# Two decoder layers without a loop: one program for both, with the memory's blocks of layer 1 in the end of layer 0

## The chip, the core and the metric

The kernel runs on one core of a Trainium2 chip. Its engines each run their own instruction stream and meet only through semaphores: TensorE (PE; its weight loads are listed as PEld), VectorE (DVE), ScalarE (ACT), GpSimd (POOL, used here for DMA issues only) and SyncE (SP, DMA issues only). The metric is the device time of one launch in microseconds (us).

## What is computed

The reference is one step of a hybrid decoder trunk of DEPTH = 2 layers, for 256 prompt tokens and 8 sample tokens together (264 columns). Cut to what matters for the change, one layer is

```
h = x @ w_in                                  # 2048 -> 19024 columns, split among the branches
mk, mv = split(mem_prompt @ w_mem_kv)         # 256 memory tokens; mem_prompt is the same in both layers
y_e = attention(mem_q, mk, mv) * silu(mem_z)  # needs mk, mv; the other branches don't
y_a .. y_d = delta net, sparse attention, retention, LRU, each times silu of its gate path
merged = sum over branches of sigmoid(gate_b) * (y_b @ w_branch[b])
out = merged @ w_out
x = LayerNorm(1.414 * x + out)                # over the 2048 features; the next layer's x
```

x of layer 0 is the input, the last x is the main output, and each layer also stores caches and states. What layer 1 needs of layer 0 is x alone; mk and mv of layer 1 need only mem_prompt and the weights.

## The kernel before

**Stages.** The program has three parts in a row: a small block that brings x in (lines 500 to 537), a hardware loop over the two layers (Fori, line 541) whose body is one block for all engines, and a small block that puts x out (lines 2133 to 2164). Between them, and at the end of each pass of the loop, stands clear_sems (line 491): all engines meet, the DMA queues are reset, all semaphores are set to zero, and all meet again. No weight of layer 1 is asked for before that.

**The stream of chunks.** The work of a layer is a list, CHUNKS (plan(), line 84), in one order for all engines: 4 chunks of mem_q (MQ), 2 "narrow", 8 "mem" (the products with w_mem_kv), then the other projections, the gates, and 16 "out" chunks (w_out). A chunk is one 128-wide column block against all 2048 rows, in 16 k-steps. x is held in features by tokens (xsplit) as a high and a low part in a rounded type, weights likewise (wsplit), and a k-step of an ordinary chunk is three products, lines 619 to 621. Before them ACT rounds a half of the weight block (line 1158) and DVE takes the rest (line 1404); SP loads the halves into a ring of four (line 572) as slots come free. A mem chunk takes its weights from the ring as they are, as float32: lines 608 (keys, 4 chunks) and 611 (values, 4 chunks). Its input memT is mem_prompt with features down, made in each layer by 32 transposes on PE (line 701) from a 2 MB load (memrow, line 1214), issued by ACT.

**The order on each engine** is written out by hand: fill(n) runs the next n k-steps of the stream on PE between the small products of a branch, stream(n) the next n chunks; ACT and DVE have stream calls of their own that prepare weights for the next chunk and empty the result banks. PSUM has four banks for the stream (mb) and four for the branches (bb).

**End of a layer.** After the last out chunk PE sums the new x over features with 16 products against ones (line 1130), DVE subtracts the mean (line 2006), ACT squares (line 1371), PE sums the squares (line 1135), ACT takes the root (line 1373), DVE the reciprocal (line 2009), DVE scales (line 2011), ACT writes the high part of the next x (line 1376) and DVE the low part (line 2015).

**Start and end of the program.** x comes in by SP: all constant tables (1551.5 KB), x_prompt (2048 KB), x_sample and the page table, then 48 transposes (lines 518 and 519), each group of three emptied by ACT and DVE. The last block adds the two parts of x (line 2150), transposes in 12 groups of four (line 2144), copies (line 2156) and stores from SP (lines 2161 and 2163).

Of the kernel before, what the change touches and what calls it, by code (L numbers as in the profile page):

```python
# [83 lines left out]
def plan():  # L84
# [20 lines left out]
CHUNKS = plan()  # L105
# [21 lines left out]
MEMKV_READY, NARROW_READY = (FREED[FIRST_RESULT[max(i for i, x in enumerate(CHUNKS) if x[0] == kind)]][1]  # L127
                             for kind in ("mem", "narrow"))


# [20 lines left out]
def kv_count(n, i):  # L151

    g = 4 if i % NKV >= 2 else 0
    return 16 * (i // NKV + 1) if n == 0 else 16 * (4 + g) + 32 * (i // NKV + 1)


def gath_count(j):

    return 16 * (4 + j // 2 + 1)


def ready(slot):

    return FREED[FIRST_RESULT[CHUNKS.index(("in", slot, CPS - 1))]][1]


# [82 lines left out]
def trunk(nc, a, o, at, fixed_w):  # L249

    n_pool = a.cache_dsa_k.shape[1]
    with ExitStack() as ctx:
# [51 lines left out]
        r1 = area(RK, 0, D)  # L304
        r2 = area(DQ, 0, W)
        memrow = area(GQ, 0, 2 * D).rearrange("p (t n) -> p t n", t=2)
        memT = area(DK, 0, KC * NMEM).rearrange("p (c n) -> p c n", n=NMEM)
        xrow = memrow
        pti = area(DK, 0, 1 + NB * NPG).bitcast(I32)
# [5 lines left out]
        def hi(ap):  # L315

            return ap.bitcast(F32R)
# [26 lines left out]
        lcount = sm(1)  # L344
# [84 lines left out]
        def kvb(n, b):  # L429
# [39 lines left out]
            ln_sum ln_cen ln_sq ln_ss ln_rs ln_x y_out se_ok mean_ok memv_out lc_ok decays_in v_chain a_chain  # L469
            cp_out""".split()  # L470
# [8 lines left out]
        layer_sems = kv_in[0:2] + list(sem) + w_landed + bw_landed + gath + stin  # L479

# [10 lines left out]
        def clear_sems():  # L491
            nc.all_engine_barrier()
            nc.gpsimd.dma_reset()
            nc.all_engine_barrier()
            for i, s in enumerate(layer_sems):
                (nc.sync, nc.scalar, nc.tensor, nc.vector)[i % 4].sem_clear(s)
            nc.all_engine_barrier()


        with nc.Block() as block:  # L500
            @block.sync
            def _(sp):
                sp.dma_start(tab[:, :], a.fixed).then_inc(sem.tables, 16)
                sp.dma_start(xrow, a.x_prompt.rearrange("a (t p) n -> p (a t) n", p=P)).then_inc(sem.x_in, 16)
                sp.dma_start(r1[0:NB, :], a.x_sample.rearrange("b t n -> (b t) n")).then_inc(sem.x_in, 16)
                pt = a.page_table.rearrange("b g -> (b g)")
                sp.dma_start(pti[:, 0:1], pt.rearrange("(p o) -> p o", o=1)).then_inc(sem.pages_in, 16)
                sp.dma_start(pti[:, 1:], pt.partition_broadcast(P)).then_inc(sem.pages_in, 16)

            @block.tensor  # L510
            def _(pe):
                pe.wait_ge(sem.tables, 16)
                pe.wait_ge(sem.x_in, 32)
                for c in range(KC):
                    if c >= 4:
                        pe.wait_ge(sem.x_ok, c - 3)
                    for t in range(2):
                        pe.transpose(mb[:, c % 4, t * P:(t + 1) * P], xrow[:, t, c * P:(c + 1) * P], ident)
                    pe.transpose(mb[:, c % 4, NP:T], r1[0:NB, c * P:(c + 1) * P], id8).then_inc(sem.x_T, 1)

            @block.scalar
            def _(act):
                for c in range(KC):
                    act.wait_ge(sem.x_T, c + 1)
                    act.activation(hi(xsplit[:, 0, c, :]), mb[:, c % 4, 0:T], ACT.Copy).then_inc(sem.xh_ok, 1)
# [1675 lines left out]
```

## Time and profile before

| | us |
|---|---|
| median of 3 runs (3160.26 to 3162.92) | 3162.58 |
| the profiled execution | 3162.21 |
| its span, first to last instruction | 3160.4 |
| PE busy | 2932.9 |
| DVE busy | 1705.0 |
| ACT busy | 974.4 |

The profile is of one execution, and sums are made against its 3162.2 us; it stands 0.4 us from the median. Busy time of PE is the union of its matmul intervals, which overlap one another; a float32 product of 256 columns stands as two records.

### The profile page before, as it was taken

The numbers are of one execution on the slowest core, as the hardware profiler recorded it, in microseconds if no ns is written. First come the engines' busy times: TensorE is split into PE (matmuls) and PEld (weight loads), VectorE is DVE, ScalarE is ACT, GpSimd is POOL, SyncE is SP. The second block draws the span as 40 slices with busy tenths as digits, with TensorE's granted clock in tenths as the row PEclk, the third lists the DMA queues.
The fourth block names the chain that finished last, engine by engine and source line by source line (L and its number), as shares of the span: only waits on it lengthen the run. The fifth ranks groups of instructions, "written<-read, shape, count | busy, mean of one in ns | idle before, by whom it ended". The sixth has DMA issues, their size and how long they took to land. (4 is left out here: it accounts for less than half of the span.)

```text
span 3160.4 us, 52449 instructions
## 1 busy us (share of the span) xinstructions
PE 2932.9 (93%) x21616; PEld 2752.6 (87%) x21616; DVE 1705.0 (54%) x2464; ACT 974.4 (31%) x1301; POOL 181.4 (6%) x204
## 2 busy tenths in 40 slices
PE   6999988999999999999779999899999999999995
PEld 5988888998999898899779888789898999989994
DVE  3155376656566747444422644765666657554444
ACT  2133332223252332223313333322233423322242
POOL 0000000000000003100000010000100000040000
PEclk9998999999999999999989999999999999999998
DMA  5576444465656567665257654444656564586651
GB/s 174 149 206 183 130 110 108 115 163 139 176 158 163 146 169 208 181 174 167 67 154 201 184 169 120 121 109 115 171 156 161 155 179 135 156 238 170 171 162 39
DMA packets 830708, 485.98 MB, mean 154 GB/s; under 512 B 26052, under 2 KB 812612, under 8 KB 829218
## 3 DMA queue, kind: packets, MB, share of 16 engines
q1 hardware_dynamic: 809328, 410.00, 48.1%
q0 software_dynamic: 19840, 66.75, 6.8%
q10 hardware_dynamic: 1296, 5.80, 0.5%
q8 instruction: 174, 2.85, 0.4%
q14 instruction: 70, 0.57, 0.1%
HBM read 466.27 MB, written 16.47 MB: 153 GB/s over the span
## 5 line engine op out<-in xcount | busy, mean ns | idle before, releaser
L619 PE MATMUL mb<-xsplit,wsplit 128*128 128x264 f32 (+1 forms) x5312 | 1580.9, 298 | 83.1 <-DVE wsplit L1404 75.9
L620 PE MATMUL mb<-xsplit,wsplit 128*128 128x264 f32 (+1 forms) x5312 | 1529.6, 288 | 0.0
L621 PE MATMUL mb<-xsplit,wsplit 128*128 128x264 f32 (+1 forms) x5312 | 1527.9, 288 | 0.0
L619 PEld LDWEIGHTS mb<-xsplit,wsplit 128*128 128x128 f32 (+1 forms) x5312 | 1022.6, 193 | 121.2 <-issue 56.0
L620 PEld LDWEIGHTS mb<-xsplit,wsplit 128*128 128x128 f32 (+1 forms) x5312 | 1022.6, 193 | 8.1 <-issue 3.8
L621 PEld LDWEIGHTS mb<-xsplit,wsplit 128*128 128x128 f32 (+1 forms) x5312 | 1016.2, 191 | 1.1
L1404 DVE TENSOR_TENSOR wsplit<-ring,wsplit 128x1024 fp32r<-128x1024 f32 (+2 forms) x664 | 776.8, 1209 | 265.8 <-ACT wsplit L1158 253.1
L1158 ACT ACTIVATE wsplit<-ring 128x1024 fp32r<-128x1024 f32 (+2 forms) x664 | 662.9, 1043 | 144.0 <-PE mb L621 99.9
L1185 ACT ACTIVATE gbuf<-mb 128x264 f32<-128x264 f32 x160 | 62.4, 390 | 840.2 <-PE mb L621 827.4
L635 PE MATMUL mb<-work,bring 128*128 128x264 f32 x1280 | 310.6, 385 | 0.0
L1434 DVE TENSOR_TENSOR gbuf<-gbuf,mb 128x264 f32<-128x264 f32 x128 | 54.8, 428 | 431.7 <-PE mb L635 424.2
L635 PEld LDWEIGHTS mb<-work,bring 128*128 128x128 f32 x1280 | 231.3, 189 | 31.6
L1199 ACT ACTIVATE work<-mb 128x264 f32<-128x264 f32 x136 | 52.8, 388 | 567.2 <-PE mb L621 562.1
L1438 DVE SCALAR_TENSOR_TENSOR work<-work,mb 128x264 f32<-128x264 f32 x32 | 13.7, 429 | 101.2 <-PE mb L621 101.2
L1688 DVE SCALAR_TENSOR_TENSOR work<-bb,mws 128x1024 f32<-128x1024 f32 x16 | 19.6, 1224 | 74.0 <-PE bb L851 74.0
L1435 DVE TENSOR_TENSOR merged<-merged,gbuf 128x264 f32<-128x264 f32 x128 | 55.4, 433 | 4.4
L611 PEld LDWEIGHTS mb<-ring,work 128*128 128x128 f32 x512 | 57.5, 192 | 0.1
L611 PE MATMUL mb<-ring,work 128*128 128x128 f32 x512 | 57.5, 275 | 0.0
L2050 POOL DMA_INDIRECT work<-in_cache_dsa_k_dram,rowsU x32 | 38.0, 1189 | 311.6 <-DVE rowsU L1997 301.3
L608 PE MATMUL mb<-work,ring 128*128 128x256 f32 x256 | 55.6, 379 | 0.0
L608 PEld LDWEIGHTS mb<-work,ring 128*128 128x128 f32 x256 | 48.5, 190 | 6.5
L749 PE MATMUL bb<-work,tab 8*128 8x512 f32 x64 | 40.6, 742 | 10.2 <-DVE work L1574 10.2
(446 smaller groups left out, 2262.6 us busy)
## 6 DMA issues: line engine op xcount, KB each, us to landing
ring<-in_w_in_dram SPq DMA_DIRECT2D x592, 512.0 KB, 4.6
bring<-in_w_branch_dram SPq DMA_DIRECT2D x160, 256.0 KB, 3.1
ring<-in_w_out_dram SPq DMA_DIRECT2D x64, 512.0 KB, 4.1
ring<-in_w_mem_kv_dram SPq DMA_DIRECT2D x32, 512.0 KB, 3.6
work<-in_cache_mem_k_dram POOLq DMA_DIRECT2D x16, 512.0 KB, 5.4
work<-in_cache_mem_v_dram POOLq DMA_DIRECT2D x16, 512.0 KB, 4.5
work<-in_mem_prompt_dram ACTq DMA_DIRECT2D x2, 2048.0 KB, 11.7
work<-in_state_gdn_dram POOLq DMA_DIRECT2D x8, 512.0 KB, 6.4
```

What stands on the lines that cost most here:

```text
L608: mm = pe.matmul(bank[:, 0:NMEM], w, memT[:, q, :], start=first, stop=last)
L611: mm = pe.matmul(bank[:, t * P:(t + 1) * P], memT[:, q, t * P:(t + 1) * P], w, start=(first and t == 0), stop=last, skip_group_check=True)
L619: pe.matmul(bank[0:n, 0:T], wh, ah, start=first, stop=False)
L620: pe.matmul(bank[0:n, 0:T], wh, al, start=False, stop=False)
L621: mm = pe.matmul(bank[0:n, 0:T], wl, ah, start=False, stop=last)
L635: mm = pe.matmul(mb[:, (g + 1) % 4, 0:T], bring[:, j % 2, q, :], y[:, q, :], start=(q == 0), stop=(q == CPS - 1))
L1158: act.activation(hi(wsplit[:, s % 4, 0, :, 0:n]), ring[:, p % NRING, :, 0:n], ACT.Copy)\
L1185: act.activation(gbuf[:, :], src[:, 0:T], ACT.Sigmoid).then_inc(sem.gate_act, 1)
L1199: act.activation(H(x)[:, m, :], src[:, 0:T], ACT.Silu if x in (GZ, DZ, RZ, LZ, MZ) else ACT.Copy).then_inc(sem.stored, 1)
L1404: dve.tensor_tensor(hi(wsplit[:, s % 4, 1, :, 0:n]), ring[:, p % NRING, :, 0:n], wsplit[:, s % 4, 0, :, 0:n], ALU.subtract).then_inc(sem.l ...
L1434: v(dve.tensor_tensor(gbuf[:, :], gbuf[:, :], proj, ALU.mult))
L1435: dve.tensor_tensor(merged[:, m, :], merged[:, m, :], gbuf[:, :], ALU.add).then_inc(sem.merged_ok, 1)
```

## The change

The two layers are written one after the other in one block, with no loop, no meeting of the engines and no clearing of semaphores: every wait gets a count that goes on over both layers (K[l], base). The two blocks that brought x in and out are parts of the same block now. CHUNKS is the list of both layers, and the 8 mem chunks are the first of each layer.

In layer 0, mem_prompt is loaded first, by SP, right behind the first 128 columns of the tables (the identity matrix); the rest of the tables follows behind the first four weight loads. x is loaded by ACT. PE transposes mem_prompt, then x, with four k-steps of mem chunks behind each group of x. At the end of layer 0, mem_prompt is loaded again behind ACT's first out chunk; its 32 transposes stand behind out chunk 3, in eight groups with four k-steps of out chunks behind each; the 16 sums of x each stand three chunks behind; and mem chunks of layer 1 (6 k-steps, then 3 behind each group of squares) stand within the norm. The last x isn't split; ACT writes it in place, PE transposes each quarter as it comes, and POOL stores it in five DMAs.

```
+    chunks.extend(("mem", 0, m) for m in range(2 * CPS))
     project(MQ)
     chunks.extend(("narrow", 0, m) for m in range(2))
-    chunks.extend(("mem", 0, m) for m in range(2 * CPS))
...
-CHUNKS = plan()
+LEN = len(plan())
+CHUNKS = plan() * DEPTH
...
-        with nc.Fori(0, DEPTH) as l:
...
+                sp.dma_start(tab[:, 0:P], a.fixed[:, 0:P]).then_inc(sem.tab_id, 16)
+                sp.dma_start(memrow, a.mem_prompt.rearrange("a (t p) n -> p (a t) n", p=P)).then_inc(sem.mem_in, 16)
...
+                        if i == 1:
+                            sp.dma_start(tab[:, P:], a.fixed[:, P:]).then_inc(sem.tables, 16)
...
+                        if kind == "mem" and m == 0:
+                            pe.wait_ge(sem.memT_ok, K[l].memT_ok + 8)
...
+                                if i % LEN == 2 * CPS:
+                                    pe.wait_ge(sem.x_ok, KC * l + q + 1)
...
+                def bring_memory(l):
+                    pe.wait_ge(sem.mem_in, K[l].mem_in + 16)
+                    for t in range(2):
+                        for q in range(4):
...
+                            for c in range(4):
+                                mm = pe.transpose(bb[:, n % 4, c * P:(c + 1) * P],
+                                                  memrow[:, t, (4 * q + c) * P:(4 * q + c + 1) * P], ident)
+                            mm.then_inc(sem.mem_T, 1)
+                            if l:
+                                fill(4)
+                bring_memory(0)
+                pe.wait_ge(sem.x_in, 32)
+                for c in range(KC):
+                    pe.wait_ge(*((sem.memT_ok, c + 5) if c < 4 else (sem.x_ok, c - 3)))
+                    for t in range(2):
+                        pe.transpose(bb[:, c % 4, t * P:(t + 1) * P], xrow[:, t, c * P:(c + 1) * P], ident)
+                    pe.transpose(bb[:, c % 4, NP:T], xsrow[:, c * P:(c + 1) * P], id8).then_inc(sem.x_T, 1)
+                    fill(4)
+                pe.wait_ge(sem.x_ok, KC)
+                pe.wait_ge(sem.tables, 16)
...
-                    stream(None)
-                    pe.wait_ge(sem.out_ok, KC)
+                    out_0 = (l + 1) * LEN - KC
+                    stream_to(out_0 + 4)
+                    if l + 1 < DEPTH:
+                        bring_memory(l + 1)
+                        pe.wait_ge(sem.memT_ok, K[l + 1].memT_ok + 8)
                     for q in range(KC):
-                        mm = pe.matmul(bb[:, 0, 0:T], ones, xnew[:, q, :], start=(q == 0), stop=(q == KC - 1))
+                        stream_to(min(out_0 + q + 3, out_0 + KC))
+                        pe.wait_ge(sem.out_ok, KC * l + q + 1)
+                        mm = pe.matmul(bb[:, 0, 0:T], ones, xnew[:, q, :], start=(q == 0), stop=(q == KC - 1),
+                                       skip_group_check=True)
                     mm.then_inc(sem.ln_sum, 1)
+                    fill(6)
                     for q in range(4):
...
                         mm.then_inc(sem.ln_ss, 1)
+                        fill(3)
+                n = 0
+                for q in range(4):
+                    pe.wait_ge(sem.xh_ok, base.xh_ok + 4 * q + 4)
...
# ACT, head of each layer
+                    stream(4)
+                    act.wait_ge(sem.x_ok, KC * (l + 1))
+                    act.wait_ge(sem.cols_ok, 1)
+                    params(l)
+                    stream(2 * CPS)
# ACT, end of each layer
+                    stream_to(out_0 + 1)
+                    if l + 1 < DEPTH:
+                        act.dma_start(memrow, a.mem_prompt.rearrange("a (t p) n -> p (a t) n", p=P)).then_inc(sem.mem_in, 16)
+                    stream_to(out_0 + KC)
# DVE, end of each layer
+                    stream_to(out_0 + 4)
+                    if l + 1 < DEPTH:
+                        bring_memory(l + 1)
+                    stream_to(out_0 + KC)
# POOL, end of the program
+                for q in range(4):
+                    pool.wait_ge(sem.x_ok, base.x_ok + 3 * q + 3)
+                    c = slice(q * 512, (q + 1) * 512)
+                    pool.dma_start(y_prompt[:, :, c], yrow[:, :, c]).then_inc(sem.y_out, 16)
+                pool.dma_start(o.y_sample.rearrange("b t n -> (b t) n"), ysrow[0:NB, :]).then_inc(sem.y_out, 16)
```

In the rows that follow, xN is a count of equal instructions, and the bracket holds the semaphores that the instruction waits for. PE at the start of the program before: the transposes of x, the meeting point (ISA, 39 semaphore clears), and the first products with weights.

```order
L518 MATMUL mb<-tab,work 128x128 [waits x_in,tables]
L518 MATMUL mb<-tab,work 128x128
L519 MATMUL mb<-tab,work 128x8
...
L496 ISA x38
L541 UNCONDITIONAL_BRANCH [waits barrier_Pool_Activation_PE_DVE_SP_release]
L584 UNCONDITIONAL_BRANCH
L619 MATMUL mb<-xsplit,wsplit 128x264 [waits lo_ok]
```

The same place now: L657 are transposes of mem_prompt, L669 and L670 of x, L596 the k-steps of mem chunks.

```order
L657 MATMUL bb<-tab,work 128x128 [waits mem_in,tab_id]
L657 MATMUL bb<-tab,work 128x128 x15
...
L669 MATMUL bb<-tab,work 128x128 [waits memT_ok,x_in]
L669 MATMUL bb<-tab,work 128x128
L670 MATMUL bb<-tab,work 128x8
L596 MATMUL mb<-work,ring 128x256 [waits w_landed0,memT_ok]
L596 MATMUL mb<-work,ring 128x256 x3
```

The mem chunks moved from behind the narrow ones to between the groups of x, and the meeting point is gone. PE at the end of layer 0 before: the sums of x (L1130), the sums of squares (L1135), the meeting point.

```order
L1130 MATMUL bb<-work,tab 128x264 [waits out_ok]
L1130 MATMUL bb<-work,tab 128x264 x15
L1135 MATMUL bb<-work,tab 128x264 [waits ln_sq]
L1135 MATMUL bb<-work,tab 128x264 x3
...
L553 UNCONDITIONAL_BRANCH
L496 ISA [waits barrier_Pool_Activation_PE_DVE_SP_release]
L496 ISA x38
```

The same place now: three of the 16 sums (L1146) are left behind the last out chunk, and k-steps of mem chunks of layer 1 (L596) stand behind them and behind each group of squares (L1153).

```order
L1146 MATMUL bb<-work,tab 128x264 [waits out_ok] x3
L596 MATMUL mb<-work,ring 128x256 [waits w_landed0,out_ok,memT_ok]
L596 MATMUL mb<-work,ring 128x256 x5
L1153 MATMUL bb<-work,tab 128x264 [waits ln_sq]
L1153 MATMUL bb<-work,tab 128x264 x3
L596 MATMUL mb<-work,ring 128x256 x2
L596 MATMUL mb<-work,ring 128x256 [waits w_landed1]
```

ACT at the same place now: behind the last scaling of x (L1431) it empties four mem chunks (L1224) ahead of the loads of the parameters, which wait for all of x.

```order
L1427 ACTIVATE work<-bb,tab 128x264 [waits ln_ss]
L1431 ACTIVATE xsplit<-work,pT 128x264 [waits ln_x] x16
L1224 ACTIVATE memkv<-mb 128x256 [waits chunk_mm] x4
L1240 DMA work<-in_conv_w_dram 4x2048 [waits cols_ok,x_ok]
L1242 DMA work<-in_conv_b_dram 1x2048
```

Before, the meeting point stood behind the scaling, and behind it the first loads and roundings of weights.

## Rows read from the trace of the kernel before

**Rows 1.** The page: span, PE's busy time, the queue of PE's instructions (packets, MB, share).
```profile
span 3160.4 us, 52449 instructions
PE 2932.9 (93%) x21616; PEld 2752.6 (87%) x21616; DVE 1705.0 (54%) x2464; ACT 974.4 (31%) x1301; POOL 181.4 (6%) x204
...
q8 instruction: 174, 2.85, 0.4%
```

**Rows 2.** Who PE waited for: total us, times, longest.
```profile
PE mb L619 <- DVE wsplit L1404: 75.9, 18, 33.4
PE mb L2144 <- DVE work L2150: 26.7, 1, 26.7
```

**Rows 3.** Timeline of PE, start: start us, us, operation, [idle before <- releaser].
```profile
13.52 0.66 PE L518 MATMUL mb<-tab,work 128*128 128x128 f32 x2 [13.52 <-DMA work<-in_x_sample_dram]
...
40.31 0.59 PE L619 MATMUL mb<-xsplit,wsplit 128*128 128x264 f32 x1 [13.63 <-DVE wsplit L1404]
```

**Rows 4.** DMA from 0 to 34 us in 40 equal slices: rate.
```profile
GB/s 0 0 146 190 380 438 409 398 410 414 434 424 453 292 82 22 0 0 0 0 0 0 0 0 0 0 0 0 0 0 0 0 0 0 0 0 0 10 10 0
```

**Rows 5.** DMA issues from 34 to 80 us: KB each, median us to landing.
```profile
ring<-in_w_in_dram SPq DMA_DIRECT2D x8, 512.0 KB, 6.2
work<-in_mem_prompt_dram ACTq DMA_DIRECT2D x1, 2048.0 KB, 11.8
```

**Rows 6.** Busy time by stretch, layer 0's head: length, PE busy (x), others, clock, DMA.
```profile
40.31:65.69 25.38, 25.38 (x192) 25.24 (x192) 8.85 (x9) 8.09 (x12) 0.00 (x0) 1.00 1.05 283
65.69:72.81 7.12, 7.12 (x69) 5.58 (x69) 2.31 (x4) 1.53 (x3) 0.00 (x0) 1.00 0.51 143
72.81:76.40 3.59, 3.59 (x34) 3.38 (x33) 2.95 (x5) 0.38 (x1) 0.00 (x0) 1.00 0.25 62
76.40:82.27 5.87, 5.87 (x52) 5.87 (x50) 1.92 (x4) 0.00 (x0) 0.00 (x0) 1.00 0.00 0
82.27:109.89 27.62, 27.62 (x130) 24.32 (x129) 0.00 (x0) 1.54 (x4) 0.00 (x0) 1.00 0.45 133
109.89:138.48 28.59, 28.59 (x258) 28.59 (x257) 3.06 (x6) 3.65 (x6) 0.00 (x0) 1.00 0.52 147
138.48:151.11 12.63, 12.63 (x106) 12.42 (x104) 3.08 (x4) 6.07 (x7) 0.73 (x1) 1.00 0.89 230
```

**Rows 7.** Timeline of POOL and DVE, first stores of the memory's keys in layer 0.
```profile
146.53 0.73 POOL L2028 DMA_DIRECT2D out_p_mem_k_dram<-stg  x1 [145.82 <-DVE stg L1535]
...
151.78 0.69 DVE L1535 COPY stg<-bb 128x512 f32<-128x512 f32 x1 [6.03 <-DMA out_p_mem_k_dram<-stg]
```

**Rows 8.** Timeline from layer 0 to layer 1: PE, then DVE and SP.
```profile
1546.40 7.39 PE L1130 MATMUL bb<-work,tab 128*128 128x264 f32 x32 [0.52 <-DVE work L1438]
1556.25 9.07 PE L1135 MATMUL bb<-work,tab 128*128 128x264 f32 x32 [2.46 <-ACT work L1371]
1598.74 0.59 PE L619 MATMUL mb<-xsplit,wsplit 128*128 128x264 f32 x1 [33.42 <-DVE wsplit L1404]
...
1574.18 6.55 DVE L2015 SCALAR_TENSOR_TENSOR xsplit<-work,pT,xsplit 128x264 fp32r<-128x264 f32 x16
...
1590.73 13.56 SPq L572 DMA_DIRECT2D ring<-in_w_in_dram  x8
```

**Rows 9.** PE in 5.8 us behind two equal waits: length, busy (records), clock, DMA.
```profile
1452.84:1458.64 5.80, 5.80 (x48) 1.00 0.01 2
3004.72:3010.52 5.80, 5.80 (x26) 0.50 0.00 1
```

**Rows 10.** Timeline of the program's end: DVE, SP, PE.
```profile
3120.72 6.55 DVE L2011 SCALAR_TENSOR_TENSOR work<-work,pT 128x264 f32<-128x264 f32 x16
...
3150.44 4.36 DVE L2156 COPY work<-mb 128x512 f32<-128x512 f32 x7 [0.16 <-PE mb L2144]
...
3152.45 0.40 SPq L2161 DMA_DIRECT2D out_y_prompt_dram<-work  x1
...
3145.02 8.26 PE L2144 MATMUL mb<-tab,work 128*128 128x128 f32 x48 [26.69 <-DVE work L2150]
```

More of the change, by code:

```diff
@@ L489, in chain, with at_l @@
             return link
[L491 to L497, printed above, removed]
+        K = [counts(l) for l in range(DEPTH)]
+        def at_l(ap, l):
+            n = len(ap.shape)
+            rest = " ".join(f"x{i}" for i in range(1, n))
+            return ap[l:l + 1].rearrange(f"z {rest} -> (z x1) " + " ".join(f"x{i}" for i in range(2, n)))
         with nc.Block() as block:
@@ L502, in _ @@
             def _(sp):
[L503 to L519, printed above, removed]
@@ new lines, in _, with weights @@
+                sp.dma_start(memrow, a.mem_prompt.rearrange("a (t p) n -> p (a t) n", p=P)).then_inc(sem.mem_in, 16)
+                def weights(l):
+                    w = {"mem": a.w_mem_kv, "out": a.w_out, "in": a.w_in}
+                    w = {name: at_l(ap, l).rearrange("(k p) n -> p k n", p=P) for name, ap in w.items()}
+                    return w, at_l(a.w_branch, l).rearrange("b (k p) n -> p b k n", p=P)
+                for l in range(DEPTH):
+                    by_kind, w_branch = weights(l)
+                    for i, (kind, x, m) in list(enumerate(CHUNKS))[l * LEN:(l + 1) * LEN]:
@@ L562, in _ @@
                             n = P
-                        w = {"mem": w_mem, "out": w_out}.get(kind, w_in)
+                        w = by_kind.get(kind, by_kind["in"])
                         for h in range(2):
@@ L805, in _ @@
                     mm.then_inc(sem.gt_mm, 1)
-                    pe.wait_ge(sem.gt_ok, 1)
+                    pe.wait_ge(sem.gt_ok, base.gt_ok + 1)
                     def rotate(n, slot, mat):
-                        pe.wait_ge(sem.stored, ready(slot))
+                        pe.wait_ge(sem.stored, ready(l, slot))
                         for c in range(CPS):
@@ new lines, in _ @@
+                        fill(3)
+                n = 0
+                for q in range(4):
+                    pe.wait_ge(sem.xh_ok, base.xh_ok + 4 * q + 4)
+                    for t in range(3):
+                        m = P if t < 2 else NB
+                        if n >= 4:
+                            pe.wait_ge(sem.x_ok, base.x_ok + n - 3)
+                        for c in range(4):
+                            mm = pe.transpose(mb[0:m, n % 4, c * P:(c + 1) * P], xnew[:, 4 * q + c, t * P:t * P + m], ident)
+                        mm.then_inc(sem.x_T, 1)
+                        n += 1
@@ new lines, in _ @@
+                act.dma_start(xrow, a.x_prompt.rearrange("a (t p) n -> p (a t) n", p=P)).then_inc(sem.x_in, 16)
+                pt = a.page_table.rearrange("b g -> (b g)")
+                act.dma_start(pti[:, 0:1], pt.rearrange("(p o) -> p o", o=1)).then_inc(sem.pages_in, 16)
+                act.dma_start(pti[:, 1:], pt.partition_broadcast(P)).then_inc(sem.pages_in, 16)
+                for c in range(KC):
+                    act.wait_ge(sem.x_T, c + 1)
+                    act.activation(hi(xsplit[:, 0, c, :]), bb[:, c % 4, 0:T], ACT.Copy).then_inc(sem.xh_ok, 1)
@@ L1216, in _ @@
+                for l in range(DEPTH):
+                    base = K[l]
                     stream(4)
+                    act.wait_ge(sem.x_ok, KC * (l + 1))
+                    act.wait_ge(sem.cols_ok, 1)
+                    params(l)
+                    stream(2 * CPS)
                     stream(2)
-                    stream(8)
                     stream(2)
@@ L1892, in _ @@
                     normed(4, RQ)
-                    dve.wait_ge(sem.stored, ready(RZ))
+                    dve.wait_ge(sem.stored, ready(l, RZ))
                     dve.tensor_tensor(H(RZ), H(RZ), H(RQ), ALU.mult).then_inc(sem.yc_ok, 1)
```

1026 lines of the change are left out of this document (505 added, 521 removed).

## The prediction

> **What bounds the kernel now.** I read the page's busy line first: PE is busy 2932.9 of 3160.4 us, no other engine over 54% [rows 1]. So the question is when PE stands still, and the list of PE's waits answers it: most of them are 1 to 6 us inside the layers, and three are not. 33.4 us of the wait for rounded weights is one wait, and 26.7 us another [rows 2]. The timelines place them. From 0 to 40.3 us PE does nothing but 48 transposes of x: 13.5 us until x has landed and 13.6 us between the last of them and the first weights [rows 3]. From layer 0 to layer 1 the last out chunk ends at 1546.40 - 0.52 = 1545.9 and the first chunk of layer 1 starts at 1598.7, 52.9 us in which PE has two runs of sums, 7.4 and 9.1 us [rows 8]; x is complete at 1580.7, and the meeting point takes from there to 1590.7, when SP asks for the first weights. At the end of the program x is scaled at 3120.72 + 6.55 = 3127.3, and the span ends at 3160.4 [rows 1, 10]. The change aims at these three places and at little else, so I sum each place as a path on PE, before and after.
>
> **Start, up to the first attention of layer 0.** Before, PE is ready for it at 151.1 and starts when the second row copy is done, 151.78 + 0.69 = 152.5 [rows 6, 7]. After, the path is:
> - First transpose. Before, tables and x (1551.5 + 2048 + 64 + 64 KB) landed by 13.5 at some 0.42 MB per us [rows 3, 4]. After, identity and memory (64 + 2048 KB) go by SP and x_sample and x (64 + 2048 KB) by ACT at the same time. If the queues share evenly, 0.5 MB more than before are in front: 13.5 + 1.2 = 14.7. If the memory comes first: 2.16 MB / 0.42 = 5.1, with some 2.9 us before the rate is reached, about 8.0. Rows 5 are the nearest: the memory on ACT's queue took 11.8 us beside weights on SP's, that is, it shared. I take 14.7.
> - The Trainium skill, page "DMA: Bandwidth & Descriptors", section "Queues, rings and completion order", has each DMA engine go round-robin between the queues with work, a packet at a time. By it loading x on a second queue buys the memory nothing, and the sum would be 14.7 too; by memory first the end would be 6.7 us earlier. No row here shows two large loads alone on two queues.
> - 32 transposes of the memory at the end block's pace of 8.26 / 48 = 0.17 us (the half clock) [rows 10]: 5.5, and 0.7 for DVE's last copy. 20.9.
> - 64 k-steps of the key chunks, 27.6 [rows 6], with 48 transposes of x between them at 3.59 / 32 = 0.11, 5.4, and the half clock at the first dense work, 25.4 - 4 x 5.8 = 2.2, as the first four chunks had it [rows 6]. 56.1. ACT and DVE emptied 16 such groups of x before in 40.31 - 13.52 - 13.63 = 13.2 us, 0.8 a group [rows 3], and now have 33 / 16 = 2.1; ACT empties the banks before it waits for x and issues the parameters, so nobody is queued behind those.
> - Value chunks 28.6, four MQ chunks 23.2, parameters and narrow chunks 7.1 + 5.9, rows and two MZ chunks 12.6 [rows 6]: 133.5.
> - The copy that PE waited for before hangs on a store of 5.3 to 6.0 us behind a late weight split [rows 7]. After, the chunk before it is a narrow one, whose weights are small and early, so the copy comes before PE needs it; I take its 1.4 us as gone.
> Gain 152.5 - 133.5 = 19.0 us.
>
> **Layer 0 to layer 1.** Before: 52.9 us from the last out chunk to MQ, and from MQ to the attention as in layer 0, 152.5 - 40.3 = 112.2; together 165.1. After, nothing of PE's work goes, it is put elsewhere: 32 transposes, 3.6, and 13 of 16 sums at 7.39 / 16 = 0.46, 6.0, stand among the out chunks, which are bound by PE, so both lengthen that stage by their own time. Behind the last chunk 3 sums, 1.4 (DVE's 0.5 lies beside two of them). Then the squares 7.4 and all 8 mem chunks 56.2, MQ 23.2 without the half clock, 7.1 + 5.9 + 12.6. Sum 3.6 + 6.0 + 1.4 + 7.4 + 56.2 + 48.8 = 123.4. Gain 41.7 us.
>
> It holds if the norm is covered. From the end of the first sums, 1553.8, to x complete took 26.9 us [rows 8]; the k-steps put between the squares make that about 29. PE reaches MQ, the first that needs x, only after 7.4 + 56.2 = 63.6. The four stream banks are the nearer limit: PE can run four mem chunks, 27.6 + 7.4 = 35, before ACT must have emptied one, and ACT is free when it has scaled x: DVE's low parts, the step behind, began 1574.2 - 1553.8 = 20.4 after the sums [rows 8], with the k-steps put between about 23. Cover left: some 12 us; each us beyond that costs one. What else is moved: the 2 MB load is issued about one out chunk into the stage, 11.8 us to land [rows 5], and PE wants it three to four chunks, 17 to 23 us, later; beside weights at 512 KB per 2.9 us the weights will be slowed, as they were to 6.2 us in rows 5, where PE didn't wait either. DVE gets 8 copies of about 0.65 us [rows 10] in two out chunks of 5.8 us, beside its own rounding there. I cost both at nothing; without cover the copies are 5 us and the load 2 to 3 us.
>
> **End.** Up to the scaling all is as before, but 0.5 us earlier (7.9 us for wait and sums become 6.0 + 1.4). Before, 3160.4 - 3127.3 = 33.1 us follow: low parts, meeting point, sum of parts, transposes, copies, one 2 MB store. After, PE transposes each quarter while DVE still scales, so 12 copies at 0.62 to 0.69 [rows 10] follow, 7.9, then on POOL two issues of 0.73 and a landing; 256 KB by POOL took 5.3 [rows 7], the last 512 KB and x_sample may take 4 to 8. 7.9 + 1.5 + 5.3 = 14.7. Gain 33.1 - 14.7 + 0.5 = 18.9.
>
> **Sum.** 19.0 + 41.7 + 18.9 = 79.6; 3162.2 - 79.6 = 3082.6, against a profiled time that stands 0.4 below the median. I say 3083. Unknown sizes: the landing at the start, 7 less or 1 more; the last store, 1 less or 3 more; the half clock within the layers. Two equal waits of 3.6 us were followed by 48 products in 5.8 us at the full clock in one layer, and by 26 at half in the other [rows 9], so a shift of all later work deals these stretches anew, each worth some 5.8 x 22 / 48 = 2.7 us; I take it as 0, plus or minus 10 (four stretches either way).
>
> **Rivals.**
> - The start runs cold, or starves. Before, PE stayed at the half clock through the 13 us of x's transposes, and transposes now stand between the k-steps. If that whole stage stays at half, 27.6 + 5.4 = 33 become 66 less the 2.2 counted: 3083 + 31 = 3114. Against: PE has no gap there, and in the first four chunks dense work warmed it within 25.4 us at a loss of 2.2 [rows 6]. Late weights behind the memory would cost up to 5: 3088. Price range 3098 to 3115.
> - More than I count: the memory lands first (6.7), the end's store lands early (1), and the anew dealt half clock comes out well (8): 3083 - 16 = 3067.
> - Slower than before. A straight program has twice the instructions to be brought in from memory. If the loop's second pass found its code on the core, PE's 174 loads of code would be more than before, and from 79.6 / 174 = 0.46 us of stall at each the gain is lost; at 1 us each the time is 3083 + 174 = 3257. Against: 2.85 MB over PE's 2 x 21616 matmul and weight instructions is 66 bytes each [rows 1], so both passes are brought in already, and PE still is busy 93%.
> - It doesn't do what it says: a wait left in the order ties layer 1's mem chunks to x, and the norm stays bare. Then the middle gain shrinks to the meeting point and the weights, 10 + 8 us, and the time is 3083 + 24 = 3107. In the order of the new kernel the mem chunks wait for banks, weights and memT alone, so little speaks for it.
>
> **How the numbers follow.** Forecast (3070 to 3097) 0.65; start costs more or norm partly bare (3097 to 3120) 0.16; more (3055 to 3070) 0.14; slower 0.03; within 0.2% of before 0.02. 0.2%, 6.3 us, is about what a measurement of this kernel can tell from no change. Likeliest 3083; the range reaches from 3063 to 3107. Faster 0.95, same 0.02, slower 0.03.
>
> **What the new profile would show.** Right: first transpose at 14 to 15 us; PE's first MQ chunk at about 85; no wait of PE over 2 us between the last out chunk of layer 0 and MQ of layer 1, with 56 us of mem chunks there; x of layer 1 complete some 30 us before MQ asks for it; the span ending 14 to 16 us after the last scaling. Wrong: PE at the half clock over most of the start, a wait of PE for stored or for the memory's landing at the layers' border, or more time in the middle of a layer than before, where the change moves nothing.

## The result

The changed kernel takes 3084.5 us (median of 4 runs, 3081.6 to 3087.0) against 3162.2 before: a ratio of 0.9755, 95% interval 0.9738 to 0.9772. The forecast was 3083, range 3063 to 3107. The page of the profile after, to set beside [rows 1]:

```profile
span 3081.8 us, 49873 instructions
...
PE 2923.6 (95%) x21616; PEld 2746.5 (89%) x21616; DVE 1693.9 (55%) x2442; ACT 970.3 (31%) x1299; POOL 184.6 (6%) x209
...
q8 instruction: 171, 2.80, 0.4%
```

PE has the same 21616 matmuls, its busy time fell by 9.3 us, and the span by 78.6. So some 69 us are time in which PE stood still. The code loaded on q8, PE's by its size, didn't grow (171 packets against 174), though the program is written out twice. Who PE waited for, after (us in total, times, longest):

```profile
PE mb L609 <- DVE wsplit L1459: 27.8, 14, 3.1
...
PE bb L657 <- DMA work<-in_mem_prompt_dram: 13.8, 1, 13.8
...
PE mb L1166 <- ACT work L1431: 4.7, 1, 4.7
```

The 33.4 and 26.7 us of [rows 2] are gone; what is left for rounded weights is 14 waits of at most 3.1 us inside the layers. Cut at the same places in both traces, the span moves like this:

| stretch (us) | before | after | gain | forecast |
|---|---|---|---|---|
| start to first attention of layer 0 | 152.5 | 134.8 | 17.7 | 19.0 |
| on to the first out chunk of layer 0 | 1300.3 | 1299.7 | 0.6 | 0 |
| on to the first attention of layer 1 | 258.7 | 216.1 | 42.6 | 41.7 |
| on to the first out chunk of layer 1 | 1293.2 | 1294.5 | -1.3 | 0 |
| on to the last scaling of x | 122.6 | 122.1 | 0.4 | 0.5 |
| on to the span's end | 33.1 | 14.5 | 18.6 | 18.4 |
| sum | 3160.4 | 3081.8 | 78.6 | 79.6 |

The stretches are differences of starts and ends in PE's and DVE's timelines.

**Start.** The timeline of PE, then the queues from 0 to 14 us (packets, MB, share of time):

```profile
13.84 6.45 PE L657 MATMUL bb<-tab,work 128*128 128x128 f32 x32 [13.84 <-DMA work<-in_mem_prompt_dram]
...
21.24 1.99 PE L596 MATMUL mb<-work,ring 128*128 128x256 f32 x8 [0.57 <-DVE work L1505]
...
86.02 0.37 PE L609 MATMUL mb<-xsplit,wsplit 128*128 128x264 f32 x1
```

```profile
q1 hardware_dynamic: 620, 2.27, 44.1%
q10 hardware_dynamic: 437, 2.17, 38.9%
```

Up to the landing of the memory SP's queue (q1) and ACT's (q10, the one with x) had moved the same amount: the two loads shared. PE was at its first MQ product at 86.0, where it had been at 40.3, but with all eight mem chunks behind it.

**Border.** Windows of PE by stage (length, PE busy and instructions, the other engines, clock, DMA): key chunks at the start, out chunks of layer 0, norm, key chunks and value chunks of layer 1, MQ.

```profile
20.13:57.52 37.39, 36.82 (x178) 29.72 (x177) 8.11 (x20) 7.07 (x19) 0.00 (x0) 1.00 0.48 151
...
1434.52:1537.14 102.62, 102.52 (x826) 101.46 (x827) 49.13 (x56) 33.01 (x32) 0.00 (x0) 1.00 0.60 172
1537.14:1552.22 15.08, 15.08 (x71) 12.84 (x70) 5.18 (x5) 5.61 (x5) 0.00 (x0) 1.00 0.12 36
1552.22:1573.37 21.15, 21.15 (x100) 18.62 (x98) 14.82 (x33) 8.00 (x20) 0.00 (x0) 1.00 0.50 150
1573.37:1601.87 28.50, 28.50 (x257) 28.50 (x256) 2.45 (x2) 3.58 (x6) 0.00 (x0) 1.00 0.62 176
1601.87:1625.26 23.39, 23.39 (x196) 23.25 (x194) 7.63 (x8) 7.87 (x12) 0.00 (x0) 1.00 0.78 186
```

PE is busy from the first out chunk to MQ without a wait and at the full clock, where [rows 8] had 33.4 us of nothing. ACT there:

```profile
1555.30 6.60 ACT L1431 ACTIVATE xsplit<-work,pT 128x264 fp32r<-128x264 f32 x16 [2.40 <-DVE work L2090]
1561.81 0.62 ACT L1224 ACTIVATE memkv<-mb 128x256 f32<-128x256 f32 x2
...
1573.57 0.38 ACT L1224 ACTIVATE memkv<-mb 128x256 f32<-128x256 f32 x1 [6.52 <-PE mb L596]
```

ACT has emptied the first bank by 1562.1, and PE wants it at 1573.4, when the fifth mem chunk begins: a cover of 11.3 us.

**End.** DVE's scaling and copies, then POOL's last stores:

```profile
3060.73 6.56 DVE L2090 SCALAR_TENSOR_TENSOR work<-work,pT 128x264 f32<-128x264 f32 x16
3067.20 7.31 DVE L2103 COPY work<-mb 128x512 f32<-128x512 f32 x12
...
3074.80 0.72 POOL L2224 DMA_DIRECT2D out_y_prompt_dram<-work  x1 [1.08 <-DVE work L2103]
3075.52 0.55 POOL L2225 DMA_DIRECT2D out_y_sample_dram<-work  x1
```

7.2 us of copies, 1.6 of issues and waits, 5.7 from the last issue to the span's end, 14.5 together. Of the 5.7, the trace's semaphore records give 3.1 to the landing of the last store, at 3079.1. The other 2.7 lie behind it: POOL is in a DRAIN instruction, which no view counts as busy, at the end of its program until 3081.6, and the other engines wait for it there.

### The profile page after: what moved, and what is told of

It reads as the page before. It is cut to its first block, busy times and chain, and to the rows that moved or that the text cites. A ratio compares the mean times of both kernels' runs of the same rounds, so it can differ in the third digit from the quotient of the medians.

```text
span 3081.8 us, 49873 instructions
## 1 busy us (share of the span) xinstructions
PE 2923.6 (95%) x21616; PEld 2746.5 (89%) x21616; DVE 1693.9 (55%) x2442; ACT 970.3 (31%) x1299; POOL 184.6 (6%) x209
## 4 chain that ended last, share of the span: by engine, by line
PE 81%; DVE 14%; ACT 3%; issue 1%; DMA 1%; POOL 0%; DVEq 0%; POOLq 0%; ACTq 0%; SPq 0%
PE mb L609 18%; PE mb L610 18%; PE mb L611 18%; PE mb L625 8%; DVE wsplit L1459 3%; PE mb L596 2%; PE mb L599 2%; DVE work L1817 1%; PE bb L1024 1%; PE bb L863 1%; PE bb L868 1%; PE bb L760 1%; DVE work L1807 1%; PE bb L971 1%; ACT wsplit L1190 1%
## 5 line engine op out<-in xcount | busy, mean ns | idle before, releaser
L596 PE MATMUL mb<-work,ring 128*128 128x256 f32 x256 | 60.3, 386 | 0.6 <-DVE work L1505 0.6
L596 PEld LDWEIGHTS mb<-work,ring 128*128 128x128 f32 x256 | 47.3, 190 | 6.8 <-DVE work L1505 0.7
```

The costliest lines, as they stand in the source:

```text
L596: mm = pe.matmul(bank[:, 0:NMEM], w, memT[:, q, :], start=first, stop=last)
```

## The experiments

The question after such a result is whether the sum came out for its own reasons. Each kernel was timed beside the kernel before (medians 3162.0 to 3164.6). Runs of one kernel spread over 2 to 13 us, so effects of a few us are read from the stage of the profile that they concern.

### The straight program alone

The order of the chunks and the k-steps put between x's groups, the sums and the squares are undone; the single program is kept.

```
-    chunks.extend(("mem", 0, m) for m in range(2 * CPS))
     project(MQ)
     chunks.extend(("narrow", 0, m) for m in range(2))
+    chunks.extend(("mem", 0, m) for m in range(2 * CPS))
...
-                    fill(4)
...
-                    fill(6)
...
-                        fill(3)
```

> The straight program alone: the mem chunks go back behind the narrow ones in both layers, nothing of the stream stands between the groups of x at the start nor in the norm; one program, early loads, the transposes of the memory and the new end stay. Theory: at the start x takes 8.4 us behind the memory's transposes, then 112.2 - 3.6 us to the first attention, 138 to 140 against 134.8, 4 to 5 later; at the border MQ starts with the first low parts of x, about 22 us behind the last out chunk, and 108.6 plus 1 for DVE's pace plus 2 to 3 for the half clock follow, 133 to 136 against 113.6, 20 to 22 later. Sum 24 to 27 us slower than the changed kernel, so that the order of the mem chunks is worth about a third of the gain and the straight program two thirds. Rival (the meeting point and the late weights are small beside the norm): 40 us and more slower.

Measured: 3109.6 us (3107.0 to 3111.8), 25.1 slower than the changed kernel. PE at the start and at the border:

```profile
32.24 0.56 PE L609 MATMUL mb<-xsplit,wsplit 128*128 128x264 f32 x1 [2.99 <-DVE wsplit L1456]
...
1566.54 0.56 PE L609 MATMUL mb<-xsplit,wsplit 128*128 128x264 f32 x1 [9.49 <-DVE xsplit L2092]
```

MQ starts 20.8 us behind the last out chunk, at its first low part of x; the first attention of layer 1 comes 130.6 behind it against 113.5, 17.1 later (20 to 22 were expected), that of layer 0 at 141.7, 6.9 later (4 to 5 expected; the memory landed 1.3 later in this run, and MQ waited 3.0 for DVE's rounding). Both stages missed their ranges, one each way, so that the total of 24 to 27 came out in part by luck. So of 78 us the single program, with its early loads, early transposes and new end, brings 53, the order of the mem chunks with its k-steps 25. The rival, 40 or more for the order, is out. No run takes the parts of the 53 apart.

### The norm's cover

In the first kernel the mem chunks stay ahead of x, but no k-step stands between the sums and squares. In the second PE also waits for all of layer 1's x (the + lines).

```
-                    fill(6)
...
-                        fill(3)
+                    if l + 1 < DEPTH:
+                        pe.wait_ge(sem.x_ok, KC * (l + 2))
```

> No k-steps of mem chunks behind the sums and between the groups of squares at the layers' border; the mem chunks follow right behind the squares, still ahead of x. Theory: from the end of the sums the squares take 2.5 + 9.1 = 11.5 us as before the change, against 13.7 with 16 k-steps in them that are worth 6.9 us, so the first MQ chunk of layer 1 comes 4.7 us later. Rival (the waits between squares are hidden anyway or followed by a half clock): 0, or 7 and more.

> As the kernel without k-steps between the squares, and PE waits for all of layer 1's x before its first mem chunk: the norm stands bare, with the straight program, early weights and early transposes kept. Theory: 27 us from the sums' end to x complete, then 56.2 us of mem chunks, 83 to 85 us to the first MQ chunk against 63.4: 20 to 22 us slower. Rival (most of the middle gain is the meeting point and the late weights, not the norm's cover): under 10 us slower.

Measured: 3084.9 (3081.2 to 3090.5) and 3106.2 us (3101.9 to 3110.2). PE, first kernel, then second (the row of mem chunks goes on past the stretch read here):

```profile
1535.14 9.08 PE L1152 MATMUL bb<-work,tab 128*128 128x264 f32 x32 [2.47 <-ACT work L1423]
1544.06 16.14 PE L596 MATMUL mb<-work,ring 128*128 128x256 f32 x74
```

```profile
1541.99 7.39 PE L1152 MATMUL bb<-work,tab 128*128 128x264 f32 x32 [2.46 <-ACT work L1425]
1564.85 3.77 PE L596 MATMUL mb<-work,ring 128*128 128x256 f32 x8 [15.47 <-DVE xsplit L2095]
```

From the last out product to MQ of layer 1 the three kernels need 64.9 (the change), 69.1 and 85.0 us. The first difference, 4.3, is the expected 4.7; the second, 20.1, is the 20 to 22 of a bare norm, 15.5 of it one wait for the last low part of x. The first kernel's total is nevertheless unchanged: its stretch from MQ to the out chunks of layer 0, where it doesn't differ from the changed kernel, took 1342.4 instead of 1348.5 us. That stretch is the subject of the next section but one.

### How much cover is left

ACT is kept busy ahead of its first emptying in layer 1.

```
+                    for _ in range(40 if l else 0):
+                        ch(act.activation(gbuf[:, :], xnew[:, 0, :], ACT.Copy))
                     stream(4)
```

> The changed kernel, and ACT writes 40 times 264 columns to a buffer that nobody reads before it empties the first mem chunk of layer 1, some 16 to 18 us in which it is not free; the result is untouched. Theory (the four stream banks are the nearest limit of the cover, ACT is free 11 us before PE wants the first bank back): the first 11 us cost nothing, the rest costs one for one, the first MQ chunk of layer 1 comes 5 to 7 us later against the last out chunk, 70 to 72 instead of 64.9. Rival (another slack stands behind, or the cover is already used up): 0, or the full 16 to 18.

Measured: 3091.9 us (3087.6 to 3097.9). ACT, then PE, and the window of the value chunks:

```profile
1557.17 18.15 ACT L1264 ACTIVATE gbuf<-work 128x264 f32<-128x264 f32 x40
```

```profile
1575.79 4.39 PE L599 MATMUL mb<-ring,work 128*128 128x128 f32 x19 [6.89 <-ACT memkv L1224]
```

```profile
1575.79:1606.40 30.61, 30.61 (x257) 30.61 (x257) 2.45 (x2) 3.93 (x8) 0.00 (x0) 0.93 0.52 147
```

18.15 of delay less 11.3 of cover are 6.9, and the wait is 6.89. The stretch to MQ grew by more than this, to 74.0 from 64.9 (70 to 72 were expected): behind the wait the value chunks took 30.6 instead of 28.5 us, at a mean granted clock of 0.93, that is, partly at 1.2 GHz. Here 6.9 us past the cover cost 9.1.

### Clock stretches within the layers

This is read from the traces of all kernels. At the first out chunk PE waits the same 3.56 us in both layers. The 5.8 us behind, layer 0 and layer 1 of the changed kernel:

```profile
1434.52:1440.32 5.80, 5.80 (x48) 5.80 (x49) 5.62 (x5) 4.33 (x5) 0.00 (x0) 1.00 0.78 320
2945.15:2950.95 5.80, 5.80 (x36) 5.80 (x37) 5.63 (x5) 4.44 (x5) 0.00 (x0) 0.74 0.02 5
```

48 products in one, 36 in the other; before it was 48 and 26 [rows 9]. Busy time times (1 - clock), summed over 5 us windows of the whole span, is 91.6 us before and 87.0 after, without the starts, where no clock is on record (see the last experiment). The stretch from MQ to the out chunks of layer 0 holds the same work in the changed kernel and in eleven of those built from it; it took between 1342.4 and 1348.5 us. The busy time lost in it at the lower clock goes from 38.3 to 46.5 us, and without this loss 1301.0 to 1304.4 us are left: most of the spread is the clock. So the forecast's "plus or minus 10" for stretches dealt anew is real: 6 us over half the program, and it hides any single edit worth less.

### Groups of x in one block

```
                     pe.transpose(bb[:, c % 4, NP:T], xsrow[:, c * P:(c + 1) * P], id8).then_inc(sem.x_T, 1)
-                    fill(4)
```

> The 16 groups of x's transposes stand in one block ahead of the mem chunks, with no k-steps between them. Theory (k-steps cover what ACT and DVE need per group): the block takes 16 x 0.8 = 13 us, then 27.6 of key chunks, 40.8 against the 36.3 of the interleaved stretch, so the first MQ chunk comes 4.5 us later and the time grows by 4 to 5 us, 2 more if the first dense stretch runs at the half clock. Rival (mixing transposes and k-steps slows both as much as it covers): within 1 us.

Measured: 3080.1 us (3077.8 to 3080.2). Windows of the block and of the key chunks:

```profile
17.93:26.40 8.47, 8.44 (x50) 5.27 (x48) 7.39 (x18) 5.87 (x15) 0.00 (x0) 1.00 0.99 307
26.40:55.06 28.66, 27.73 (x129) 24.43 (x130) 0.97 (x4) 1.54 (x4) 0.00 (x0) 1.00 0.43 129
```

8.5 + 28.7 = 37.1 us against the interleaved 37.4: the rival holds, the interleaving buys nothing. A group of x costs PE 0.53 us in the block and about (37.4 - 27.6 - 0.6) / 16 = 0.58 between k-steps. The 0.8 us on which I counted was PE's own pace in the kernel before, whose clock rose only at 44.7 us, in the first dense work; ACT and DVE keep up with 0.53 as well. The 4 us by which the time is lower are not the edit's: 1.1 are an earlier landing and 1.2 shorter transposes of the memory, where the clock rose earlier, both ahead of it, and the rest lies within the layers.

### Which load lands first

x goes to SP's queue behind the memory; in the second kernel the page table follows it there (the last three lines), so that ACT's queue is empty.

```
                 sp.dma_start(memrow, a.mem_prompt.rearrange("a (t p) n -> p (a t) n", p=P)).then_inc(sem.mem_in, 16)
+                sp.dma_start(xsrow, a.x_sample.rearrange("b t n -> (b t) n")).then_inc(sem.x_in, 16)
+                sp.dma_start(xrow, a.x_prompt.rearrange("a (t p) n -> p (a t) n", p=P)).then_inc(sem.x_in, 16)
+                pt = a.page_table.rearrange("b g -> (b g)")
+                sp.dma_start(pti[:, 0:1], pt.rearrange("(p o) -> p o", o=1)).then_inc(sem.pages_in, 16)
+                sp.dma_start(pti[:, 1:], pt.partition_broadcast(P)).then_inc(sem.pages_in, 16)
```

> x_sample and x are loaded by SP's own queue, behind the memory, instead of by ACT's at the same time. Theory (two queues share the transfer rate evenly, so the memory waits for x): the memory lands as if alone, 2.16 MB at 0.42 MB per us and 2.9 us before the rate is reached, so PE's first transpose goes from 13.8 to about 8.0 us, the first MQ chunk from 86.0 to about 80.5, the time falls by 5.5 us. Rival (the order of queues doesn't matter, the landing is set by something else): first transpose stays at 13 to 14 us and the time within 1 us.

> As the kernel with x behind the memory on SP's queue, and the page table's two loads (64.5 KB in pieces of 512 bytes and less) also on SP's queue, behind x, so that ACT's queue is empty. Theory (the page table's small pieces, then alone on ACT's queue, took turns with the memory's and held the rate at 160 to 300 GB/s in the first 7 us): the memory lands 8.0 us behind its issue as at the layers' border, first transpose at 9.2 to 9.5 us against 11.6 there and 13.8 in the changed kernel. Rival (one queue alone can't bring the rate up sooner): first transpose at 11 to 12 us.

Measured: 3083.3 (3079.5 to 3084.7) and 3080.8 us (3075.1 to 3088.4); first transposes at 11.6 and 10.1 us, first MQ at 83.7 and 83.3. The landings expected (8.0, then 9.2 to 9.5) were missed, and so was the first kernel's MQ at 80.5; its median is 1.2 us lower, not 5.5. DMA issues up to 14 us (KB, us to landing), first kernel, then second, and a wait of PE in the second:

```profile
work<-in_mem_prompt_dram SPq DMA_DIRECT2D x1, 2048.0 KB, 10.2
...
merged<-in_page_table_dram ACTq DMA_DIRECT2D x1, 64.0 KB, 7.7
```

```profile
work<-in_mem_prompt_dram SPq DMA_DIRECT2D x1, 2048.0 KB, 8.8
```

```profile
PE mb L601 <- DMA ring<-in_w_mem_kv_dram: 1.5, 1, 1.5
```

Sharing with x was a reason for 13.8, but not all of it goes at once: with x out of the way the memory landed 10.2 us after its issue instead of 12.5, with the page table out of the way too 8.8, 0.8 more than expected. That the page table's 64.5 KB cost the last 1.4 us isn't shown: it is one execution against another, and the seven kernels whose loads at the start are alike spread as far, from 11.5 to 12.9. In the second kernel the weights, queued behind x and the page table, were late by 1.5, so that this step brought nothing at MQ. The Trainium skill, page "DMA: Bandwidth & Descriptors", section "Queues, rings and completion order", has the DMA engines take turns between queues a packet at a time; the 2.27 and 2.17 MB on q1 and q10 agree with it.

### What sets the end

First kernel: DVE keeps every second copy, ACT takes the others, PE has eight banks. Second: SP instead of POOL issues the stores, nothing else.

```
-                for n in range(12):
+                for n in range(0, 12, 2):
...
-                    pool.dma_start(y_prompt[:, :, c], yrow[:, :, c]).then_inc(sem.y_out, 16)
+                    sp.dma_start(y_prompt[:, :, c], yrow[:, :, c]).then_inc(sem.y_out, 16)
```

> At the program's end every second of the 12 copies goes to ACT, and PE's transposes use eight banks instead of four. Theory (DVE's 12 copies of 0.61 us, which begin when its last scaling is done, set the end): the last copy is done 2.5 to 3 us earlier, at about 4.3 instead of 7.2 us behind DVE's last scaling, and the time falls by as much. Rival (PE's transposes at the half clock or the stores set the end): within 1 us.

> The five stores of the last x are issued by SP instead of POOL. Theory (a store lands alike from either): two issues of 0.72 and 0.54 become two of 0.40, the span ends 0.5 us earlier, landing 5.7 us behind the last issue as now. Rival (POOL's way of issuing itself costs in the landing): 2 to 3 us earlier.

Measured: 3085.7 (3085.4 to 3087.7) and 3082.9 us (3079.7 to 3085.1). Copies and stores of the first kernel (span 3085.9), then the stores of the second (span 3077.8, last scaling at 3066.4):

```profile
3065.89 6.55 DVE L2099 SCALAR_TENSOR_TENSOR work<-work,pT 128x264 f32<-128x264 f32 x16
...
3074.76 1.27 DVE L2112 COPY work<-mb 8x512 f32<-8x512 f32 x2
...
3074.34 2.97 POOL L2234 DMA_DIRECT2D out_y_prompt_dram<-work  x4 [286.57 <-DVE work L2112]
3077.27 0.58 POOL L2235 DMA_DIRECT2D out_y_sample_dram<-work  x1
```

```profile
3068.22 5.75 SPq L571 DMA_DIRECT2D out_y_prompt_dram<-work  x4
3074.01 0.41 SPq L572 DMA_DIRECT2D out_y_sample_dram<-work  x1
```

My theory of the copies falls. They were done 3.6 us behind the last scaling instead of 7.2, even less than the 4.3 expected, but the end came 13.5 behind it instead of 14.5: POOL, at 0.74 an issue, put out all five stores in one row, and the last landed 5.3 behind its issue, where it had been 3.1. With SP, and the slow copies left as they are, the end came 11.4 behind the scaling, and only 3.4 behind the last issue (5.7 with POOL). The number is the rival's, 2 to 3 us, but the place isn't the landing: the last store landed 3.0 us behind its issue, against 3.1 with POOL, and the end came 0.4 behind that landing instead of 2.7. What is gone is POOL's DRAIN, which with SP's stores ends at 2788.5, 2.8 us behind POOL's last transfer and long before the span's end. In the nine traces in which POOL stores the last x the span ends 2.7 us behind the last landing, in the five in which SP does 0.4. The same page of the Trainium skill, section "Specifications", gives 1 us for the first byte by POOL's way and 0.6 by SP's; no run here shows this difference by itself. Each is one profiled execution, and the medians don't separate the two from the changed kernel.

### A version that beats both

What the last two sections point to, in one kernel; SP loads the memory in two halves, then the weights of two chunks, x and the page table; ACT and DVE empty the memory's banks in turn, and two mem chunks run ahead of x's groups. The end has both edits of the last section. The second and third kernel add products of the identity on PE ahead of the transposes, 32 and 12 of them (the diff is the third's).

```
+                for t in range(2):
+                    sp.dma_start(memrow[:, t:t + 1, :], m_rows[:, t:t + 1, :]).then_inc(sem.y_out if t else sem.mem_in, 16)
...
+                for _ in range(12):
+                    pe.matmul(bb[:, 3, 0:P], ident, ident, start=True, stop=True)
                 bring_memory(0)
+                fill(2 * KC)
...
-                    fill(4)
+                    fill(2)
```

> All loads of the start on SP's queue in the order of need: identity, the memory in two halves, the weights of two chunks, x, page table; the tables' rest behind the fourth chunk's weights. PE transposes each half as it lands, into eight banks, ACT and DVE copy in turn; two mem chunks run ahead of x's groups, two k-steps stand behind each. At the end ACT takes every second copy, PE has eight banks, SP stores. Theory (first come, first served within a queue; POOL's stores were the end's last bound): first transpose at about 7 us, all 32 done at 13.4 if they go at the 0.8 us a group seen at the start so far, first MQ chunk at about 79 instead of 86.0; the span ends 8.5 to 9 us behind DVE's last scaling instead of 14.5. 12 to 13 us faster than the changed kernel. Rival (the weights behind the memory come too late, as in the kernel with the page table behind x; the stores' transfer keeps the end): 3 to 6 us faster.

> The same, and 32 products of the identity with itself, whose results nobody reads, on PE from when the identity has landed, about 3 us, until the memory's first half. Theory (the transposes at the start go at half the pace of those at the layers' border, 0.8 us a group of four against 0.36, because PE stood idle before): the groups of the second half take 0.36 to 0.5 us, and the first MQ chunk comes 2 to 2.5 us earlier than without these products. Rival (the slow pace at the start has another reason, the writes of the landing transfers or the copies out of the banks): no earlier than without.

> As the kernel with the new start and end, with 12 products of the identity instead of 32, at 0.31 us each, so that they end at about 6.5 us, when the memory's first half lands. Theory (work on PE ahead of the transposes brings their full pace earlier): the 32 transposes take 4 to 5.5 us instead of 6.5, the first MQ chunk comes at 77 to 78 instead of 79.0, the time falls by 1 to 2 us against the kernel without these products. Rival (3.8 us of work is too little to raise the pace, or the weights, landed at 11 us, are the next limit): 79 as without.

Measured, with the ratio to the kernel before and its interval, the first MQ product, and the span's end behind the last scaling:

| kernel | median (runs), us | ratio | MQ | end |
|---|---|---|---|---|
| the change | 3084.5 (3081.6 to 3087.0) | 0.9755 (0.9738 to 0.9772) | 86.0 | 14.5 |
| no products | 3071.7 (3070.2 to 3081.1) | 0.9722 (0.9708 to 0.9735) | 79.05 | 9.6 |
| 32 products | 3077.2 (3074.7 to 3079.1) | 0.9731 (0.9718 to 0.9744) | 82.7 | 9.6 |
| 12 products | 3075.9 (3069.9 to 3079.4) | 0.9723 (0.9710 to 0.9737) | 77.1 | 9.6 |

The first kernel's median is 12.8 us below the changed kernel's, as expected (by the ratios it is 10), with 7 at the start and 5 at the end (9.6 behind the scaling, 8.5 to 9 expected). PE at the start, without products and with 12:

```profile
6.36 3.65 PE L675 MATMUL bb<-tab,work 128*128 128x128 f32 x16 [6.36 <-DMA work<-in_mem_prompt_dram]
9.80 3.03 PE L675 MATMUL mb<-tab,work 128*128 128x128 f32 x16
```

```profile
2.70 4.47 PE L683 MATMUL bb<-tab 128*128 128x128 f32 x24 [2.70 <-DMA tab<-in_fixed_dram]
7.00 1.91 PE L675 MATMUL bb<-tab,work 128*128 128x128 f32 x16
8.91 1.97 PE L675 MATMUL mb<-tab,work 128*128 128x128 f32 x16
```

The 32 transposes take 3.9 us behind 4.3 us of products, against 6.5 without: their slow pace at the start comes from PE's rest before, not from the landing transfers or the copies. It is the lower clock, as the program's end before shows, where transposes of the same size run at both levels (a window's length, PE busy, the other engines, clock):

```profile
3145.02:3150.82 5.80, 5.80 (x27) 5.80 (x28) 3.84 (x6) 0.00 (x0) 0.00 (x0) 0.50 0.00 0
3150.82:3153.01 2.19, 2.19 (x23) 1.83 (x21) 2.18 (x5) 0.00 (x0) 0.00 (x0) 1.00 0.00 0
```

From start to start they are 0.213 us apart at 0.50 and 0.109 at 1.00. At the start of the changed kernel they go from 0.213 to 0.109 at 19.5 us, the moment at which the trace's first record of the clock begins, at the full level; ahead of it there is no record, and the 1.00 of a window there says nothing. In each of the fourteen traces PE's pace doubles where that first record begins: at 12.1 us without products, at 5.9 with 12 of them, at 44.7 in the kernel before.

The 32 products were too many: at 0.31 us each they ran until 12.8 and made MQ later by 3.6. The 2 us that 12 products win at MQ don't show in the medians; against each other the first and third kernel are the same within what these runs can tell.

## Why the prediction was right, step by step

- **Where PE stood still.** Right: the three places gave 79.3 us, and the two stretches within the layers 0.6 and -1.3.
- **Start, 133.5 forecast, 134.8 measured.** The landing was 0.9 earlier than the even sharing gave, and sharing it was. The transposes of the memory took 6.3 us, not 5.5. Those of x were mis-sized: 16 groups at 0.58 are 9.2 us, not 5.4, because I took the pace of the memory's 128-wide transposes [rows 6] for groups that end in an 8-wide piece; even in one block a group took 0.53. The 2.2 us of half clock at the first dense work weren't paid, since the clock had risen at 19.5 us, in the memory's transposes, and the first k-step starts at 21.2. Errors of -0.9, 0.8, 3.8 and -2.2, with some tenths elsewhere, leave 1.3: that so little is left is luck.
- **The reason for 0.17 us a transpose.** I called it the half clock by the row of the end, and the half clock is right for the start. But 0.17 isn't its pace: the row's 8.26 us hold 27 transposes at 0.50 and the rest at 1.00, 0.213 and 0.109 us apart. The row's mean fitted a start that happened to hold both as well.
- **Border, 41.7 forecast, 42.6 measured.** Each term held: transposes and sums among the out chunks lengthened that stage by 102.6 - 93.0 = 9.6 us (3.6 + 6.0), and behind it stood no wait. The cover was put at some 12 us and was 11.3, shown by the kernel that used it up; the bare norm at 24, and it cost 20.1 (with the early weights kept).
- **End, 14.7 forecast, 14.5 measured.** Right in size by luck, wrong in its picture: I had copies of 7.9, issues of 1.5 and a landing of 5.3 in a row, and took the copies for what to cut. Copies and issues took 7.2 and 1.6, but the landing took 3.1, and 2.7 of POOL's DRAIN and the meeting of the engines behind it, at which I had put nothing, filled the rest. Halving the copies moved the end by 1.0; the stores were next.
- **The sum.** The median, 3084.5, is 1.5 us from the forecast. Equal work differs by up to 6 us over half the program, mostly by the clock, so this closeness is luck; the mechanism is borne out by the three places, not by the nearness of the total.
- **Rivals.** Starved or cold start: the key chunks ran at 1.00 with one gap of 0.6 us; only the memory's transposes ahead of them were in part at the half clock. Slower by code: 171 packets against 174, so the forecast's 0.46 us a load has no ground. A norm left bare: out by the trace, priced by experiment. More than I counted: the memory didn't land first.

## What to carry to other kernels

A straight program pays where a meeting point keeps the next stage's loads and first operands back: here two thirds of the gain came from that, and one third from putting work that doesn't depend on the late operand into the gap. Size such a cover by the first buffer that must come free, not by the amount of work: behind it the cost set in at one for one, and the clock added to it. Two loads on two queues shared the rate here; what is wanted first goes alone, with its weights, ahead of the rest on one queue. At a program's end, look at what still runs behind the last landing.

## What was not expected of the hardware

- The same 32 transposes at the start took 5.3 to 6.6 us from kernel to kernel without products ahead of them, as the clock rose earlier or later among them; after 4.3 us of products they took 3.9. A window ahead of the first record of the clock reads 1.00 there, though the pace is half.
- Transposes alone brought the clock to the full level: at 19.5 us in the changed kernel, and, with the rise on record, at 3150.8 in the kernel before. The 48 of x at the start of the kernel before, 13.1 us of them, had not: there the first record is 4.4 us into the dense work.
- POOL's DRAIN at the end of its program ended 2.5 us behind the last landing of its stores (3081.6 against 3079.1). Issued by SP, the last store landed as late behind its issue (3.0 against 3.1 us), but the span ended 0.4 us behind the landing instead of 2.7.
